# Token-major three-pass retention, and the recurrence one head later, in a two-block layer kernel

## Chip, cores and metric

One core of one Trainium2 chip. The metric is the device time of one execution in microseconds; the kernel before was run three times, 1894.63 to 1899.74 us, median 1894.76.

## What is computed

A batch of one, 512 tokens, width 1024, everything in fp32. Block one: adaptive norm, a projection into seven streams, a causal convolution and gated linear recurrence (RG-LRU), stick-breaking attention in eight heads, a gated mix, `w_out`, then a convolved GELU feed-forward. Block two: a layer with latent attention and multiscale pooling, then a retention layer and a final norm. The two pieces that the change touches:

```python
# block one, per head of 128 channels
log_a = -RG_C * r * softplus(-lam); a = exp(log_a)
u = sqrt(-expm1(2.0 * log_a)) * (i * x)
h = a_t * h + u_t                      # scan over the 512 tokens
y_a = h * gelu(yr)
...
log_beta = log_sigmoid(z)              # z = q k^T / sqrt(d)
suffix = reverse cumsum(log_1mb) - log_1mb
y_b = where(mask, exp(log_beta + suffix), 0) @ v
mix = sigmoid(ga) * y_a + sigmoid(gb) * y_b
# block two, retention, 4 heads with dk = 256, dv = 512, forward and backward decays
scores = (q k^T) * dmat ;  o = scores @ v
y = groupnorm(o) * gn_g * silu(gate) ;  y @ w_out
```

## The kernel before

The engines run hand-written queues tied by semaphores. Activations lie channel-major (channels on partitions, 512 tokens in the free dimension). The weights come as 286 *units* of up to 1024 rows by 128 columns (`UNITS`, made by `ring_plan`). SyncE loads a unit into one of three slots of `raw`, ScalarE copies it to fp32r as the high half (`split_ahead`, L852, at most two units ahead of the one it reads), GpSimd subtracts to get the low half (L478), and TensorE's `unit` (L511 to L513) multiplies in three passes per 128 rows: high by high, high by low, low by high, 24 matmuls of 512 columns for a full unit. Each unit writes a PSUM bank; `bank_plan` deals them in turns from a ring of two banks (`lin`) or, for the kinds in `WIDE`, of five, and a unit first waits until the reader of the bank's previous unit has finished (`BEFORE`, `FREED`).

Block one is a loop of nine steps h. Step h runs the seven units of head h (q, k, v, xr, yr, ga, gb) and the attention of head g = h - 1:

- TensorE: q(h), scores of g into `big` (L602), k(h), v(h), square sum of q in `m_a` (`square`, L532), xr(h), suffix sums of g (L627, L629), square sum of k, yr(h), four transposes of v(h) (L640), ga(h), gb(h), the two gate matmuls of head h (L650, L655), the product attention by v of g into `m_o` (L660). On even steps 16 one-column matmuls of the modulation (L549) stand ahead of the suffixes.
- ScalarE: Abs, Exp, Ln of the scores (L940 to L944), roots of the square sums (L864, L867), Sigmoid of ga, then Sigmoid and Tanh of the recurrence gate (L985, L987), Sigmoid of gb (L992, waits for `mixed`), of the input gate (L995), Sqrt (L999).
- VectorE: shifted logs of g and their split, five lines from L1313 to L1324; one accumulation of the modulation (L1213, weights in `ada_ring`), q norm, convolution of xr(h), L1345, k norm, mask (L1359); then it waits for `av_done` and mixes head g (L1362 to L1368); then decay and recurrence of head h (L1373 to L1394) and the last accumulation.

Step 8 holds only the attention of head 7, with the first seven eighths of the units w_out 0 and 1 laid between its pieces; their last eighth needs `mixed` of head 7.

In a retention head the units are rq, rk (2 each), rv (4), rgate (4). v comes out channel-major, ScalarE copies each unit to SBUF, four fp32 transposes turn it (L797) and ScalarE copies it back as `v_tk`. VectorE rotates q and k. The scores (L809) and the output (L817) are full fp32 matmuls:

```python
for k in range(2):
    last = nc.tensor.matmul(big[:, (4 * h + j) % 3], rk_r[:, k, j * P:(j + 1) * P], rq_r[:, k],
                            start=(k == 0), stop=(k == 1))
...
last = nc.tensor.matmul(ro_bank[b], s_sb[:, j, b * P:(b + 1) * P], v_tk[:, j],
                        start=(j == 0), stop=(j == TB - 1))
```

The scores are multiplied by the decay table on VectorE (L1668). A full fp32 matmul stands in the trace as two records.

## Time and profile before

| | |
|---|---|
| median of three runs | 1894.76 us |
| profiled execution | 1894.31 us |
| its span | 1892.5 us |
| TensorE matmul busy | 1766.3 us, 93% |
| VectorE, ScalarE, GpSimd busy | 944.1, 842.3, 681.6 us |
| mean granted TensorE clock | 0.975 |

The share of busy time is an average over stages, and a matmul's recorded end is modelled: consecutive matmuls overlap in the records, so lengths are best read from starts. Idle time in a row is the time in which the engine stood before that instruction, with what it waited for. Times in a row count from the span's start.

### The profile page before, as it was taken

Reading aid. Unit: us, or ns where it says so; the run is one execution under the profiler, and the core shown is the slowest. Engines: PE = TensorE matmul, PEld = TensorE weight load, DVE = VectorE, ACT = ScalarE, POOL = GpSimd, SP = SyncE. Lnnn points to the kernel's source line nnn. Section 1 sums busy time; section 2 is a strip of 40 time slices with the busy share of each in tenths; the row PEclk is TensorE's granted clock in tenths of the full one; section 3 lists DMA queues with packets and bytes.
Section 4 is the critical chain, followed back from the end, with each engine's and each line's share of the span. In section 5 each row is a group of like instructions: output and inputs, shape, how many; then the busy total and the mean of one; then the engine's idle time right before and its main releaser. Section 6 shows DMA issues by size and latency. Waiting matters only on the chain.

```text
span 1892.5 us, 19419 instructions
## 1 busy us (share of the span) xinstructions
PE 1766.3 (93%) x7336; PEld 1342.9 (71%) x7336; DVE 944.1 (50%) x1137; ACT 842.3 (45%) x1034; POOL 681.6 (36%) x322
## 2 busy tenths in 40 slices
PE   4999999998779999999998989999999999999997
PEld 2777777776557787788786768555578686786765
DVE  6567776666447718525523662344435252233432
ACT  3577666766234424323443321455534343233432
POOL 1333333323244444444452444112244242441424
PEclk7999999999799999999999999999999999999998
DMA  9233332322112232232221222111223121221312
GB/s 364 90 122 101 112 119 83 122 101 74 55 67 90 89 100 90 89 115 98 90 99 50 87 97 67 48 37 37 70 68 100 45 90 56 90 95 39 100 34 78
DMA packets 50350, 168.19 MB, mean 89 GB/s; under 512 B 5585, under 2 KB 10833, under 8 KB 49745
## 3 DMA queue, kind: packets, MB, share of 16 engines
q1 hardware_dynamic: 50256, 166.95, 26.3%
q8 instruction: 59, 0.97, 0.2%
q14 instruction: 35, 0.28, 0.0%
HBM read 164.83 MB, written 2.10 MB: 88 GB/s over the span
## 4 chain that ended last, share of the span: by engine, by line
PE 72%; DVE 22%; ACT 3%; issue 2%; POOL 1%; DMA 1%; SPq 0%; DVEq 0%; ACTq 0%
PE lin L511 18%; PE lin L513 17%; PE lin L512 17%; PE big L817 2%; PE big L754 2%; PE big L753 2%; PE m_o L770 1%; PE big L809 1%; DVE scr L1213 1%; PE big L511 1%; DVE cq_lo L1324 1%; DVE tmp L1375 1%; PE big L512 1%; PE big L513 1%; DVE scr L1320 1%
## 5 line engine op out<-in xcount | busy, mean ns | idle before, releaser
L478 POOL TENSOR_TENSOR w_lo<-raw,w_hi 128x1024 fp32r<-128x1024 f32 (+3 forms) x286 | 640.5, 2243 | 1161.5 <-ACT w_hi L852 1161.4
L511 PE MATMUL lin<-h_hi,w_hi 128*128 128x512 f32 x1328 | 532.7, 401 | 21.6 <-POOL w_lo L478 11.6
L513 PE MATMUL lin<-h_hi,w_lo 128*128 128x512 f32 x1328 | 518.9, 391 | 0.0
L512 PE MATMUL lin<-h_lo,w_hi 128*128 128x512 f32 x1328 | 518.2, 390 | 0.0
L852 ACT ACTIVATE w_hi<-raw 128x1024 fp32r<-128x1024 f32 (+3 forms) x286 | 277.6, 971 | 184.0 <-DVE x L1476 72.0
L511 PEld LDWEIGHTS lin<-h_hi,w_hi 128*128 128x128 f32 x1328 | 250.2, 188 | 89.6 <-POOL w_lo L478 20.5
L512 PEld LDWEIGHTS lin<-h_lo,w_hi 128*128 128x128 f32 x1328 | 250.3, 188 | 54.7 <-issue 5.0
L513 PEld LDWEIGHTS lin<-h_hi,w_lo 128*128 128x128 f32 x1328 | 250.0, 188 | 53.3
L511 PE MATMUL lin<-y_hi,w_hi 128*128 128x512 f32 x484 | 190.9, 394 | 15.3 <-DVE y_lo L1469 4.5
L513 PE MATMUL lin<-y_hi,w_lo 128*128 128x512 f32 x484 | 189.1, 391 | 0.0
L512 PE MATMUL lin<-y_lo,w_hi 128*128 128x512 f32 x484 | 188.9, 390 | 0.0
L511 PEld LDWEIGHTS lin<-y_hi,w_hi 128*128 128x128 f32 x484 | 91.2, 188 | 39.5 <-issue 6.5
L1458 DVE SCALAR_TENSOR_TENSOR scr<-lin,par,scr 128x511 f32<-128x511 f32 x96 | 72.0, 750 | 82.8 <-ACT scr L1018 62.7
L513 PEld LDWEIGHTS lin<-y_hi,w_lo 128*128 128x128 f32 x484 | 91.1, 188 | 19.2
L512 PEld LDWEIGHTS lin<-y_lo,w_hi 128*128 128x128 f32 x484 | 91.3, 189 | 18.7 <-issue 0.2
L1644 DVE TENSOR_TENSOR scr<-lin,rstd 128x512 f32<-128x512 f32 x16 | 11.1, 692 | 132.9 <-PE lin L513 132.9
L1476 DVE SCALAR_TENSOR_TENSOR x<-lin,small,x 128x512 f32<-128x512 f32 x24 | 18.0, 751 | 88.5 <-PE lin L513 88.5
L1018 ACT ACTIVATE scr<-lin,par 128x512 f32<-128x512 f32 x24 | 18.7, 780 | 82.3 <-PE lin L513 82.3
L1014 ACT ACTIVATE scr<-lin,par 128x512 f32<-128x512 f32 x24 | 18.7, 780 | 64.6 <-PE lin L513 62.0
L1702 DVE TENSOR_TENSOR x<-lin,x 128x512 f32<-128x512 f32 x16 | 11.1, 692 | 63.3 <-PE lin L513 63.3
L511 PE MATMUL big<-h_hi,w_hi 128*128 128x512 f32 x96 | 37.7, 393 | 4.7 <-POOL w_lo L478 4.7
L817 PE MATMUL big<-scr 128*128 128x512 f32 x96 | 41.9, 592 | 0.0
(276 smaller groups left out, 2350.4 us busy)
## 6 DMA issues: line engine op xcount, KB each, us to landing
raw<-weights SPq DMA_DIRECT2D x246, 512.0 KB, 3.5
ada_ring<-ada SPq DMA_DIRECT2D x32, 512.0 KB, 4.2
scr<-ada SPq DMA_DIRECT2D x16, 512.0 KB, 6.3
raw<-weights SPq DMA_DIRECT2D x16, 192.0 KB, 2.3
x<-x_t SPq DMA_DIRECT2D x2, 1024.0 KB, 6.0
out_t<-scr SPq DMA_DIRECT2D x8, 256.0 KB, 2.0
rgw<-rg_w SPq DMA_DIRECT2D x1, 1024.0 KB, 6.5
scr<-inv_counts SPq DMA_DIRECT2D x1, 1024.0 KB, 5.8
```

Of the source, the lines that this page charges most:

```text
L478: nc.gpsimd.tensor_tensor(w_lo[:, s, 0:w], raw[:, s, 0:w], w_hi[:, s, 0:w].bitcast(F32), ALU.subtract).then_inc(w_split, 1)
L511: nc.tensor.matmul(psum_of(n), wh, hi(k), start=(k == 0), stop=False)
L512: nc.tensor.matmul(psum_of(n), wh, lo(k), start=False, stop=False)
L513: last = nc.tensor.matmul(psum_of(n), wl, hi(k), start=False, stop=(k == nk - 1))
L753: nc.tensor.matmul(big[:, q % 3], qn_sb[:, cols], kn_sb[:], start=True, stop=False)
L754: nc.tensor.matmul(big[:, q % 3], qrr[rows, h // 2, cols], krr[rows], start=False, stop=True, tile_position=(64 * (h % 2), 0)).then_inc(s_ ...
L770: last = nc.tensor.matmul(m_o[:], vtok[:, g % 2, j], p_t[:, j], start=(j == 0), stop=(j == TB - 1))
L809: last = nc.tensor.matmul(big[:, (4 * h + j) % 3], rk_r[:, k, j * P:(j + 1) * P], rq_r[:, k], start=(k == 0), stop=(k == 1))
L817: last = nc.tensor.matmul(ro_bank[b], s_sb[:, j, b * P:(b + 1) * P], v_tk[:, j], start=(j == 0), stop=(j == TB - 1))
L852: nc.scalar.activation(w_hi[:, s, 0:wd], raw[:, s, 0:wd], ACT.Copy).then_inc(w_high, 1)
L1213: v.scalar_tensor_tensor(out=acc, in0=src, scalar=p_("c", k), in1=acc, op0=M, op1=AD).then_inc(ada_used, 1)
L1458: v.scalar_tensor_tensor(out=o[:, s:T], in0=psum_of(n)[:, 0:T - s], scalar=p_("ffn_conv_w", 48 * (2 - s) + half + c), in1=o[:, s:T], op0=M ...
```

## The change

**Retention.** The rv units become `value_unit`: the activations are the stationary operand and 512 weight columns move, so that v comes out token-major in four banks at once (`rv_bank`), with no transposes. q, k, v and the decayed scores are each split into a high and a low half (ScalarE copies, VectorE subtracts), and scores and output run in three passes of fp32r. The old wait for `yr_ready` is gone; the value units wait for `on_done` and `yrp_done` of the head before.

**Block one.** Head h's xr, yr, ga, gb and its recurrence move from step h to step h + 1, beside the attention of the same head. The wait for `av_done` and the mixing move behind the recurrence. Head 0's second square sum goes to `m_b`. In step 1, k stands ahead of the scores. The last head's tail is written out by itself. `w_out` joins `WIDE`, and rv units take no turn in the bank rings.

The core of the diff (the loading order of `ring_plan` follows the new order of units; the weight array of an rv unit is 256 rows by 512 columns):

```diff
-WIDE = ("kr", "cq", "ckv", "u", "pool", "pgate", "p_out")
+WIDE = ("w_out", "kr", "cq", "ckv", "u", "pool", "pgate", "p_out")
...
+        if kind == "rv":
+            continue
         ring = 5 if kind in WIDE else 2
...
+        rv_bank = [big[:, 2], m_o[:], m_a[:], m_b[:]]
...
+            def value_unit(h, c):
+                n = UNIT[("rv", 4 * h + c)]
+                s = n % NR
+                pe.wait_ge(w_split, n + 1)
+                for k in (2 * c, 2 * c + 1):
+                    at = (k % 2) * T
+                    wh, wl = w_hi[:, s, at:at + T], w_lo[:, s, at:at + T]
+                    for b in range(TB):
+                        hh, hl = h_hi[:, k, b * P:(b + 1) * P], h_lo[:, k, b * P:(b + 1) * P]
+                        nc.tensor.matmul(rv_bank[b], hh, wh, start=(k == 0), stop=False)
+                        nc.tensor.matmul(rv_bank[b], hh, wl, start=False, stop=False)
+                        last = nc.tensor.matmul(rv_bank[b], hl, wh, start=False, stop=(k == DK - 1))
+                last.then_inc(unit_done, 1)
...
+                for c in range(4):
+                    value_unit(h, c)
+                unit("rgate", 4 * h, H, L)
+                pe.wait_ge(rqk_low, 4 * h + 4)
+                pe.wait_ge(rv_low, 4 * h + 1)
...
+                        kh, kl = k_hi[:, k, j * P:(j + 1) * P], k_lo[:, k, j * P:(j + 1) * P]
+                        nc.tensor.matmul(out, kh, q_hi[:, k], start=(k == 0), stop=False)
+                        nc.tensor.matmul(out, kh, q_lo[:, k], start=False, stop=False)
+                        last = nc.tensor.matmul(out, kl, q_hi[:, k], start=False, stop=(k == 1))
                     last.then_inc(rs_scores, 1)
                 unit("rgate", 4 * h + 1, H, L)
-                pe.wait_ge(rs_done, 4 * h + 4)
-                pe.wait_ge(rvt_copied, 4 * h + 4)
+                pe.wait_ge(rs_low, 4 * h + 4)
+                pe.wait_ge(rv_low, 4 * h + 4)
...
+                        nc.tensor.matmul(ro_bank[b], sh, v_hi[:, j], start=(j == 0), stop=False)
+                        nc.tensor.matmul(ro_bank[b], sh, v_lo[:, j], start=False, stop=False)
+                        last = nc.tensor.matmul(ro_bank[b], sl, v_hi[:, j], start=False, stop=(j == TB - 1))
...
+            g = HEADS - 1
+            unit("xr", g, H, L)
+            pe.wait_ge(kq_normed, 2 * HEADS)
+            pe.wait_ge(gates_read, g)
+            scores(g)
+            unit("yr", g, H, L)
+            modulation(5)
+            pe.wait_ge(conv_done, HEADS)
+            nc.tensor.matmul(m_a[:], rgw[:, g], A(S1["xr"], g), start=True, stop=True).then_inc(gate_r_done, 1)
+            unit("ga", g, H, L)
+            pe.wait_ge(lm_done, HEADS)
+            suffixes()
+            unit("gb", g, H, L)
+            pe.wait_ge(att_t, HEADS)
+            nc.tensor.matmul(big[:, 2], rgw[:, 8 + g], A(S1["xr"], g), start=True, stop=True).then_inc(gates_done, 1)
+            for m in range(2):
+                unit("w_out", m, YH, YL, ready=None if m else lambda k: (mixed, k + 1), part=range(7))
+            pe.wait_ge(att_done, HEADS)
+            products(g)
```

VectorE in the loop of block one before, a middle head, from the mask to the next head's logs (`m_o` is the product, `tmp` the recurrence):

```order
L1359 TENSOR_TENSOR scr<-scr,cst 128x128 x4
L1362 TENSOR_TENSOR tmp<-m_o,scr 128x512
L1364 TENSOR_TENSOR tmp<-tmp,scr 128x512
L1366 CAST y_hi<-tmp 128x512
L1368 TENSOR_TENSOR y_lo<-tmp,y_hi 128x512
L1373 TENSOR_SCALAR tmp<-tmp 128x512
```

The same place in the changed kernel (line numbers are its own):

```order
L1453 TENSOR_TENSOR scr<-scr,cst 128x128 x4
L1459 TENSOR_SCALAR tmp<-tmp 128x512
L1461 RECIPROCAL tmp<-tmp 128x512
L1467 TENSOR_TENSOR tmp<-tmp,scr 128x512
L1470 SCALAR_TENSOR_TENSOR tmp<-tmp 128x512
L1473 TENSOR_TENSOR tmp<-tmp 128x512
L1475 TENSOR_SCALAR tmp<-tmp 128x512
L1477 SCALAR_TENSOR_TENSOR tmp<-tmp 128x512
L1480 TENSOR_TENSOR tmp<-tmp,scr 128x512
L1483 TENSOR_TENSOR scr<-tmp,scr 128x512
L1487 TENSOR_TENSOR tmp<-m_o,scr 128x512
L1489 TENSOR_TENSOR tmp<-tmp,scr 128x512
```

The read of `m_o` has moved from the place right behind the mask to the end of the recurrence.

VectorE in a retention head before, from the last rotation to the first statistics (L1644 scales a gate unit, L1668 is the decayed score):

```order
L1493 TENSOR_TENSOR scr<-scr,tmp 128x512
L1644 TENSOR_TENSOR scr<-lin,rstd 128x512
L1668 SCALAR_TENSOR_TENSOR scr<-big,small,tmp 128x512 x4
L1644 TENSOR_TENSOR scr<-lin,rstd 128x512
L1675 BN_STATS small<-m_o 128x6
```

And in the changed kernel (`qk_hl` holds the halves of q and k, `cq_lo` the low half of v):

```order
L1641 TENSOR_TENSOR scr<-scr,tmp 128x512
L1813 TENSOR_TENSOR qk_hl<-scr,qk_hl 128x512 x4
L1817 TENSOR_TENSOR cq_lo<-big,cq_hi 128x512
L1817 TENSOR_TENSOR cq_lo<-m_o,cq_hi 128x512
L1817 TENSOR_TENSOR cq_lo<-m_a,cq_hi 128x512
L1817 TENSOR_TENSOR cq_lo<-m_b,cq_hi 128x512
L1792 TENSOR_TENSOR scr<-lin,rstd 128x512
L1824 SCALAR_TENSOR_TENSOR tmp<-big,small,tmp 128x512 x2
L1830 TENSOR_TENSOR s_lo<-tmp,s_hi 128x512
L1824 SCALAR_TENSOR_TENSOR tmp<-big,small,tmp 128x512
```

Twelve subtractions are new in each head, and the score products alternate with four of them.

## Rows read from the trace of the kernel before

**Rows 1.** The page, busy times and costliest groups: busy, mean ns, idle before.

```profile
PE 1766.3 (93%) x7336; PEld 1342.9 (71%) x7336; DVE 944.1 (50%) x1137; ACT 842.3 (45%) x1034; POOL 681.6 (36%) x322
...
L478 POOL TENSOR_TENSOR w_lo<-raw,w_hi 128x1024 fp32r<-128x1024 f32 (+3 forms) x286 | 640.5, 2243 | 1161.5 <-ACT w_hi L852 1161.4
...
L511 PEld LDWEIGHTS lin<-h_hi,w_hi 128*128 128x128 f32 x1328 | 250.2, 188 | 89.6 <-POOL w_lo L478 20.5
```

**Rows 2.** Waits of TensorE: us in total, times, longest us.

```profile
PE big L627 <- DVE cq_lo L1324: 13.8, 7, 4.8
```

**Rows 3.** Timeline of TensorE, heads in the loop: start, us, instruction, idle before.

```profile
190.77 1.02 PE L650 MATMUL m_a<-scr,rgw 128*128 128x512 f32 x2
...
222.57 0.50 PE L627 MATMUL big<-cq_hi,sel_r 128*128 128x512 f32 x1 [2.35 <-DVE cq_lo L1324]
...
244.71 1.02 PE L650 MATMUL m_a<-scr,rgw 128*128 128x512 f32 x2
```

**Rows 4.** Timeline of VectorE, same heads, and one earlier row.

```profile
113.51 1.49 DVE L1324 TENSOR_TENSOR cq_lo<-scr,cq_hi 128x1280 fp32r<-128x1280 f32 x1
...
194.91 0.69 DVE L1362 TENSOR_TENSOR tmp<-m_o,scr 128x512 f32<-128x512 f32 x1 [9.41 <-PE m_o L660]
...
198.66 0.43 DVE L1373 TENSOR_SCALAR tmp<-tmp 128x512 f32<-128x512 f32 x1
...
211.40 1.49 DVE L1313 SCALAR_TENSOR_TENSOR scr<-big,scr 128x1280 f32<-128x1280 f32 x1
...
218.84 3.68 DVE L1324 TENSOR_TENSOR cq_lo<-scr,cq_hi 128x1280 fp32r<-128x1280 f32 x1
```

**Rows 5.** Timeline of ScalarE, same heads.

```profile
209.57 1.28 ACT L944 ACTIVATE scr<-scr 128x1280 f32<-128x1280 f32 x1
...
246.54 0.72 ACT L987 ACTIVATE tmp<-tmp,small 128x512 f32<-128x512 f32 x1
```

**Rows 6.** Windows: length, busy (x) of PE, PEld, DVE, ACT, POOL, granted clock, DMA.

```profile
125.00:446.00 321.00, 311.39 (x1347) 243.97 (x1347) 221.84 (x215) 214.23 (x229) 106.06 (x43) 0.98 0.32 107
461.00:510.00 49.00, 29.80 (x106) 22.25 (x105) 32.63 (x36) 16.68 (x16) 7.98 (x3) 0.73 0.10 32
1433.00:1870.00 437.00, 431.59 (x1790) 324.52 (x1789) 159.63 (x213) 158.57 (x200) 156.47 (x66) 1.00 0.22 70
```

**Rows 7.** Timeline of TensorE, end of the last head.

```profile
465.67 4.08 PE L602 MATMUL big<-scr 128*128 128x512 f32 x8 [4.29 <-ACT tmp L995]
...
487.90 0.79 PE L627 MATMUL big<-cq_hi,sel_r 128*128 128x512 f32 x1 [4.79 <-DVE cq_lo L1324]
...
498.95 4.64 PE L660 MATMUL m_o<-scr,vtok 128*128 128x512 f32 x8 [5.67 <-DVE scr L1359]
...
506.44 0.47 PE L511 MATMUL lin<-y_hi,w_hi 128*128 128x512 f32 x1 [2.86 <-DVE y_lo L1368]
```

**Rows 8.** Timeline of TensorE, first head, behind the v unit.

```profile
65.74 1.02 PE L532 MATMUL m_a<-sq_act,cst 128*128 128x512 f32 x2
```

**Rows 9.** Timeline of TensorE, third retention head.

```profile
1678.88 0.39 PE L511 MATMUL lin<-h_hi,w_hi 128*128 128x512 f32 x1
...
1684.33 0.60 PE L797 MATMUL m_a<-cst,scr 128*128 128x128 f32 x4
...
1690.26 0.60 PE L797 MATMUL m_b<-cst,scr 128*128 128x128 f32 x4
...
1714.86 3.59 PE L817 MATMUL m_o<-scr 128*128 128x512 f32 x8
...
1718.29 7.03 PE L817 MATMUL big<-scr 128*128 128x512 f32 x16
```

**Rows 10.** Timeline of ScalarE, table load and weight split, first retention head.

```profile
1477.05 1.28 ACT L907 ACT_TABLE_LOAD   x1 [4.39 <-DVE scr L1644]
...
1479.64 1.06 ACT L852 ACTIVATE w_hi<-raw 128x1024 fp32r<-128x1024 f32 x1
```

**Rows 11.** Timeline of VectorE, a score product, first retention head.

```profile
1478.47 0.75 DVE L1668 SCALAR_TENSOR_TENSOR scr<-big,small,tmp 128x512 f32<-128x512 f32 x1 [1.49 <-PE big L809]
```

More of the change, by code:

```diff
@@ L527, in YL, with square @@
                 return y_lo[:, k]
-            def square(count, first, last):
+            def square(count, first, last, out=m_a[:]):
                 pe.wait_ge(squared, count)
-                nc.tensor.matmul(m_a[:], c_("ones"), sq_act[:, count % 2], start=first, stop=last)\
+                nc.tensor.matmul(out, c_("ones"), sq_act[:, count % 2], start=first, stop=last)\
                     .then_inc(square_used, 1)
@@ L597, in _ @@
                     unit("q", h, H, L)
+                if h == 1:
+                    unit("k", h, H, L)
                 if g >= 0:
                     pe.wait_ge(kq_normed, 2 * g + 2)
-                    pe.wait_ge(gates_read, g + 1)
-                    for j in range(TB):
-                        last = nc.tensor.matmul(big_f[:, COL[j]:COL[j] + KW[j]],
-                                                A(S1["k"], g)[:, j * P:(j + 1) * P], A(S1["q"], g)[:, j * P:T],
-                                                start=True, stop=True)
-                    last.then_inc(z_done, 1)
-                if h == HEADS:
-                    unit("w_out", 0, YH, YL, ready=lambda k: (mixed, k + 1), part=range(7))
-                if 0 < h < HEADS:
+                    if g > 0:
+                        pe.wait_ge(gates_read, g)
+                    scores(g)
+                if h > 1:
                     unit("k", h, H, L)
@@ L658, in _ @@
                     pe.wait_ge(att_done, g + 1)
-                    for j in range(TB):
-                        last = nc.tensor.matmul(m_o[:, j * P:T], vtok[:, g % 2, j],
-                                                att_a[:, COL[j]:COL[j] + KW[j]],
-                                                start=(j == 0), stop=(j == TB - 1))
-                    last.then_inc(av_done, 1)
+                    if h < HEADS:
+                        pe.wait_ge(vt_copied, h + 1)
+                    products(g)
+            g = HEADS - 1
+            unit("xr", g, H, L)
+            pe.wait_ge(kq_normed, 2 * HEADS)
+            pe.wait_ge(gates_read, g)
+            scores(g)
+            unit("yr", g, H, L)
+            modulation(5)
+            pe.wait_ge(rgw_loaded, 16)
+            pe.wait_ge(conv_done, HEADS)
+            pe.wait_ge(rooted, 2 * HEADS)
+            nc.tensor.matmul(m_a[:], rgw[:, g], A(S1["xr"], g), start=True, stop=True).then_inc(gate_r_done, 1)
+            unit("ga", g, H, L)
+            pe.wait_ge(lm_done, HEADS)
+            suffixes()
+            unit("gb", g, H, L)
+            pe.wait_ge(att_t, HEADS)
[3 more added lines that the diff above has]
+            pe.wait_ge(att_done, HEADS)
+            products(g)
             pe.wait_ge(gates_read, HEADS)
@@ L928, in _ @@
             highs(0)
-            for h in range(HEADS + 1):
+            for h in range(HEADS):
                 g = h - 1
-                if h == HEADS:
-                    split_ahead(UNIT[("w_out", 0)])
                 if h < HEADS:
@@ L1308, in _ @@
+            for h in range(HEADS):
                 g = h - 1
```

450 lines of the change are left out of this document (274 added, 176 removed).

## Prediction

> **What bounds the kernel now.** I read the page first: TensorE is busy for 93% of the span [rows 1], and nearly all of it is three-pass units, so only two things can move the time: TensorE work that disappears, and TensorE waits (with the slow clock that follows them). Next I read the list of waits for TensorE: one line of the first block stands out, the suffix sums waiting for VectorE's last attention operand, 13.8 us in seven waits [rows 2]. The timelines of the three engines around one head [rows 3 to 5] show why, the windows [rows 6] show the clock, the timeline of the last head's end [rows 7] shows the largest hole, and that of a retention head [rows 9] shows what a matmul costs in each number format.
>
> **The change part by part.**
>
> *Retention, arithmetic.* A unit takes 5.45 us (from its start at 1678.88 to the transposes behind it at 1684.33), that is 24 reduced-precision (fp32r) matmuls of 512 columns at 0.227 us. With the four value transposes it is 5.93 (1684.33 to 1690.26), so a group of transposes costs 0.48; a full fp32 matmul is two records, and eight records take 3.43 us (1714.86 to 1718.29), 0.429 each [rows 9]. Per head the change removes 4 groups of transposes, 4 x 0.48 = 1.92. The scores were 8 fp32 matmuls, 16 x 0.429 = 6.86, and become 24 x 0.227 = 5.45: 1.41 less. The output was 16 matmuls, 32 x 0.429 = 13.72, and becomes 48 x 0.227 = 10.9: 2.82 less. The value units keep 96 matmuls of 512 columns; only which operand is stationary changes. That is 6.15 us per head, **-24.6 us** for four. No TensorE wait stands in this stage that could have swallowed it: TensorE is busy 431.6 of 437 us at full clock [rows 6].
>
> *Retention, new waits.* The scores now wait for the split q and k and for the first value bank, the output for the split scores. Let e be the end of the last value unit. ScalarE has one weight split and four copies to make, VectorE four subtractions; the first value bank is free at about e+2.5, and rgate 0 covers TensorE until e+5.44. q and k are split during the value units. Behind the scores: VectorE scales rgate 0, ScalarE loads a table (1.28) and does the silu and a weight split (1.06) [rows 10], so the first score copy ends near e+10.1. Then VectorE needs four score products (0.75) [rows 11] and four subtractions (about 0.7), ending near e+14.5 undisturbed. rgate 1 covers TensorE until e+16.3. A VectorE operation that meets GpSimd's split can grow: the last attention subtraction took 1.49 undisturbed and 3.68 in another head [rows 4], 2.2 more, which is one GpSimd operation (mean 2.243) [rows 1]. One such hit gives e+16.7. I put **+0.5 us** for the stage; two hits in every head would give 4 x 2.6 = 10, and the bound below is nothing.
>
> Were each of the four score subtractions hit, the path would grow by 4 x 2.2 against a slack of 16.3 - 14.5 = 1.8, and the stage would lose 4 x 7.0 = 28 us, all of its gain. GpSimd has only one split to make in that stretch, so I keep one hit. The Trainium skill, page "SBUF — State Buffer", section "two separate sides", says that VectorE operations with two SBUF inputs and GpSimd operations take a shared port pair as an exclusive lock for the whole instruction, so that all four are exposed; the trace agrees on the size of a hit, 2.2 us.
>
> *Head loop, heads 2 to 7.* Today VectorE sits idle 9.41 us for the products of the head before, mixes (194.91 to 198.66, 3.75 us), and only then runs decay, recurrence and one more accumulation (198.66 to 211.40, 12.7 us), and the shifted logs [rows 4]. Their last subtraction ends at 222.52 and TensorE has stood 2.35 us [rows 3]. After the change decay waits only for the tanh of the gate. It ends 2.55 us after its gate matmul starts (244.71 to 247.26) [rows 3, 5], so at 193.3 in the head shown; 12.7 + 3.75 puts the shifted logs at about 209.8. ScalarE's Ln ended at 210.85 [rows 5], but it also waited for the mixing (its sigmoid of gb) and moves up by about 1.8. So the logs start 1.6 to 2.4 us earlier, and the last subtraction leaves the GpSimd operation that it met (3.68 against 1.49). The wait goes. What these waits cost: 13.8 - 4.79 = 9.0 us in six heads, 1.0 for ends that are modelled 0.16 late, and (1 - 0.98) x 321 = 6.4 us of half clock after them [rows 2, 3, 6, 7]; 16.4 in all. The modulation's one-column matmuls stay beside the suffixes in every second head and may still lower the clock once or twice, so I take **-14.5 us** (ends -6 and -17). VectorE's products are no longer late for anybody: their wait moves behind the recurrence.
>
> *The end of the last head.* Between 461 and 510 us TensorE is idle 49 - 29.8 = 19.2 us; the clock's mean of 0.73 means 26.5 us at half speed, of which the waits of 4.79 and 5.67 hold 10.5, so 16 us of matmuls lose 8 [rows 6, 7]. That is 27.2 us over the work. The new order lays xr, yr, ga, gb (21.8 us of units that were done earlier before) between the pieces. I followed the three engines from the last loop gate matmul (t = 0). VectorE: 2.55 + 12.7 + 3.75 is 19 at the latest, against TensorE's arrival at the modulation at 16.9: 1 to 2 us of wait; the convolution then holds the gate matmul some 0.5. The shifted logs (6.7 undisturbed, 11.1 with the hits of [rows 4]) follow from 20.3: the suffixes wait 0.5 to 4.5. The last mixing must follow products and both w_out parts: about 2.9 us, as now (2.86) [rows 7]. Sum 5 to 10, with half-clock pieces 7 to 13. I take 9: **-18 us** (ends -14 and -22).
>
> *The start.* Head 0's q, k, v stand alone, the v unit ending at 65.74 [rows 8]. Then: two square sums 1.7, q and k of head 1 10.9, scores 2.15, v 5.44: TensorE asks for xr at 87. Its weight split, however, is queued on ScalarE behind Abs, Exp, Ln (three times 1.28 [rows 5] and two table loads of 1.28, from 81 to 87.4), then takes 1.06 there [rows 10] and 2.24 on GpSimd: 90.8. That is 3.8 us of new wait; the suffixes behind it may wait another 0 to 1.7, and the clock may fall: **+6.5 us** (ends +3.5 and +9). The second square sum's own bank saves nothing visible: it lets ScalarE's two roots follow each other, and they are covered by q and k.
>
> *Banks.* w_out joins the five-bank ring, which shifts the later turns: qr 0 now inherits its bank from the last p_out instead of the sixth, and waits for that residual: **+1 us**.
>
> **Sum.** -24.6 + 0.5 - 14.5 - 18 + 6.5 + 1 = -49.1. The profiled execution took 1894.31 us for a span of 1892.5, 0.45 under the median of the runs shown; so 1894.8 - 49.1 = 1845.7, say 1845.
>
> **Rivals.** *Scores split too late* (10 in 100): two GpSimd hits in every retention head, +10: 1855; with all four hit, +28: 1873 (2 in 100). For it: 3.68 against 1.49 [rows 4]. Against: one split in that stretch. *The head loop keeps its waits* (12 in 100): the recurrence, now ahead of the mixing, meets three GpSimd splits (each +2.2) and the logs start no earlier; then the head loop gives nothing and the end of the last head 14: 1845 + 14.5 + 4 = 1863 or so. For it: the same enlarged row; against: the 9.41 us of idle time that VectorE gets back. *Start and end cost less* (7 in 100): +3.5 and -22 in place of +6.5 and -18, 1838. *Weight load exposed, slower than before* (3 in 100): the value units now keep activations stationary, and the scores and outputs issue many more loads. A load takes 0.188 us [rows 1] and is hidden under the matmul today, as 0.227 per matmul shows. There are 4 x (96 + 24 + 48) = 672 such matmuls; if the load stood bare they would cost 126 us: 1971. It decides from 49/672 = 0.07 us per matmul. Against it: units already change their stationary operand with every weight half. *It nets out* (2 in 100).
>
> **How the numbers follow.** The forecast holds 64 in 100 with 1840 to 1851 of its own. To hold eight in ten the range reaches down to 1837 and up to 1860, which takes in the first rival and the middle of the second. Below 0.3% (5.7 us) two runs of this kernel can't be told apart; everything but the last two cases is faster by more: 0.95, 0.02, 0.03.
>
> **What would show it.** Retention: scores begin to rgate 1 in 5.4 us, outputs 10.9, no wait over 0.5 before the outputs. Head loop: no wait of the suffixes in heads 2 to 7, heads without modulation near 49.7 us apart, VectorE's wait for the products under 1 us. Start: one wait near 87 us for GpSimd's split of xr 0. End: four waits of which the last, before w_out's eighth block, is near 3. I would be wrong if the shifted logs are still late, if the outputs wait for split scores, or if a value unit takes more than 5.5 us.

## The result and the profile after

| | before | after |
|---|---|---|
| median | 1896.17 us (4 runs) | 1834.41 us (4 runs, 1830.78 to 1836.63) |
| ratio | | 0.9667, interval 0.965 to 0.9685 |
| profiled execution, span | 1894.31, 1892.5 us | 1834.91, 1833.1 us |
| granted clock, mean | 0.975 | 0.982 |

The change is worth 61.8 us, where 49.8 (1894.8 to 1845) were forecast; 1834.4 lies 2.6 us under the range's lower end. The span shrank by 59.4 us; the rest is scatter between executions.

The page of the changed kernel, TensorE's busy time and GpSimd's weight splits; compare [rows 1]:

```profile
PE 1728.7 (94%) x7368; PEld 1347.4 (74%) x7368; DVE 984.1 (54%) x1185; ACT 852.9 (47%) x1050; POOL 684.9 (37%) x322
L508 POOL TENSOR_TENSOR w_lo<-raw,w_hi 128x1024 fp32r<-128x1024 f32 (+3 forms) x286 | 643.8, 2254 | 1098.1 <-ACT w_hi L924 1097.8
```

The list of TensorE's waits (total us, times, longest). The line of the suffix sums, 13.8 us in [rows 2], has gone from it altogether; those below are the block-one waits that the prediction speaks of, but for the one at the start (its row stands further below), and the one of qr 0 (the third row):

```profile
PE lin L541 <- DVE y_lo L1493: 2.8, 1, 2.8
PE m_b L594 <- DVE small L1330: 1.0, 1, 1.0
PE lin L541 <- DVE x L1734: 0.9, 1, 0.9
PE m_a L734 <- issue: 0.5, 1, 0.5
```

**The six heads of the loop.** The windows of before, then of after, from the second group of value transposes to the eighth (length, busy time of each engine with its instructions, granted clock, DMA):

```profile
125.49:446.01 320.52, 310.91 (x1346) 243.65 (x1345) 221.39 (x214) 213.94 (x228) 105.95 (x43) 0.98 0.32 107
```

```profile
106.65:407.23 300.58, 300.58 (x1345) 238.56 (x1344) 207.80 (x214) 213.93 (x228) 107.99 (x43) 1.00 0.34 114
```

After, TensorE is busy for every one of the 300.58 us, at full clock. VectorE does the same 214 pieces in 13.6 us less, and the groups by line in these windows show where: the last attention subtraction, before and after (busy us, mean ns).

```profile
L1324 DVE TENSOR_TENSOR cq_lo<-scr,cq_hi 128x1280 fp32r<-128x1280 f32 x6 | 22.1, 3683 | 0.2
```

```profile
L1434 DVE TENSOR_TENSOR cq_lo<-scr,cq_hi 128x1280 fp32r<-128x1280 f32 x6 | 9.0, 1492 | 0.2
```

It grew beside GpSimd's split in all six heads and grows in none. The shifted logs of the head that answers to [rows 4], on VectorE, and TensorE's first suffix sum behind them:

```profile
187.32 1.49 DVE L1423 SCALAR_TENSOR_TENSOR scr<-big,scr 128x1280 f32<-128x1280 f32 x1
...
194.84 1.49 DVE L1434 TENSOR_TENSOR cq_lo<-scr,cq_hi 128x1280 fp32r<-128x1280 f32 x1
196.37 3.43 DVE L1326 SCALAR_TENSOR_TENSOR scr<-slab,par,scr 128x1024 f32<-128x1024 f32 x1
```

```profile
197.76 0.39 PE L651 MATMUL big<-cq_hi,sel_r 128*128 128x512 f32 x1
```

The last subtraction takes 1.49 us, as forecast; it ends at 196.33 and TensorE comes at 197.76: 1.4 us of room. In the three heads in which the modulation's matmuls stand ahead of the suffixes it is 3.1 us. GpSimd's weight split beside that subtraction, before and after:

```profile
218.80 2.37 POOL L478 TENSOR_TENSOR w_lo<-raw,w_hi 128x1024 fp32r<-128x1024 f32 x1 [1.99 <-ACT w_hi L852]
```

```profile
196.32 2.39 POOL L508 TENSOR_TENSOR w_lo<-raw,w_hi 128x1024 fp32r<-128x1024 f32 x1 [3.18 <-ACT w_hi L924]
```

Before, the split began 0.04 us ahead of the subtraction (218.84 in [rows 4]). Now it begins 0.02 us before the subtraction ends, in all six heads. In three of them the accumulation behind the subtraction grows in its place (3.43 against 1.28); in the other three VectorE has nothing to do there. The shifted logs start 4.1 us ahead of the square sum that stands before xr (187.32 and 191.41) where they started 1.95 us ahead of it (211.40 and 213.35), while ScalarE makes its half of this split behind the root of that same square sum. The mask additions met GpSimd's split before (3.50 us for four) and meet it still (3.58).

**The start and the last head**, TensorE's rows that waited (compare [rows 7]):

```profile
90.40 0.76 PE L541 MATMUL lin<-h_hi,w_hi 128*128 128x512 f32 x1 [2.49 <-POOL w_lo L508]
...
436.68 1.95 PE L594 MATMUL m_b<-cst,scr 128*128 128x1 f32 x16 [0.95 <-DVE small L1330]
439.08 2.04 PE L734 MATMUL m_a<-scr,rgw 128*128 128x512 f32 x2 [0.45 <-issue]
...
470.75 0.47 PE L541 MATMUL lin<-y_hi,w_hi 128*128 128x512 f32 x1 [2.85 <-DVE y_lo L1493]
```

The clock was 0.50 for 3.4 us behind the first and behind the third of them:

```profile
90.50:93.90 3.40, 3.40 (x8) 2.68 (x9) 3.27 (x4) 3.31 (x5) 2.23 (x1) 0.50 0.45 153
438.60:442.00 3.40, 2.95 (x6) 1.72 (x6) 3.33 (x3) 1.93 (x3) 1.69 (x1) 0.50 0.18 27
```

**Retention**, VectorE's score splits in one head, and TensorE's first output:

```profile
1658.36 2.26 DVE L1830 TENSOR_TENSOR s_lo<-tmp,s_hi 128x512 fp32r<-128x512 f32 x1 [1.09 <-ACT s_hi L1270]
...
1661.44 0.69 DVE L1830 TENSOR_TENSOR s_lo<-tmp,s_hi 128x512 fp32r<-128x512 f32 x1
...
1662.95 1.49 DVE L1830 TENSOR_TENSOR s_lo<-tmp,s_hi 128x512 fp32r<-128x512 f32 x2
```

```profile
1664.49 0.50 PE L888 MATMUL m_o<-cq_hi,s_hi 128*128 128x512 f32 x1
```

Of the four subtractions one was hit (2.26 against 0.69) in each of the four heads, as the forecast's sum has it, with 1.6 us and not 2.2. The last ends at 1664.44, and TensorE starts 0.05 us later. No idle time is listed, but the output starts 0.31 us after the matmul ahead of it (1664.18) where matmuls of one unit follow each other in 0.23: it waited for the split, by 0.08 us, in each head.

Where the 59.4 us of span are, by landmarks of both traces:

| stretch | before | after | measured | forecast |
|---|---|---|---|---|
| start (from the end of head 0's v unit to the second group of value transposes) | 36.2 | 40.4 | +4.2 | +6.5 |
| six heads of the loop | 320.5 | 300.6 | -19.9 | -14.5 |
| end of the last head (from the eighth group to the next norm's sum) | 119.7 | 97.6 | -22.1 | -18 |
| qr 0 | | | +1.1 | +1 |
| retention, from the third norm's sum to the last norm's | 448.8 | 424.6 | -24.2 | -24.1 |
| rest of the kernel | | | +1.6 | 0 |

Four units and two gate matmuls (4 x 5.45 + 2 x 0.86 = 23.5 us) have moved from the first stretch to the third. To compare the same work, they are taken off the start before (59.75 as it stands in the trace) and added to the end before (96.2).

### The profile page after: what moved, and what is told of

The parts are those of the page before. It is cut to its first block, busy times and chain, and to the rows that moved or that the text cites. A ratio compares the mean times of both kernels' runs of the same rounds, so it can differ in the third digit from the quotient of the medians.

```text
span 1833.1 us, 19563 instructions
## 1 busy us (share of the span) xinstructions
PE 1728.7 (94%) x7368; PEld 1347.4 (74%) x7368; DVE 984.1 (54%) x1185; ACT 852.9 (47%) x1050; POOL 684.9 (37%) x322
## 4 chain that ended last, share of the span: by engine, by line
PE 80%; DVE 13%; ACT 3%; issue 2%; POOL 1%; DMA 1%; SPq 0%; DVEq 0%; ACTq 0%
PE lin L541 19%; PE lin L543 18%; PE lin L542 18%; PE big L835 2%; PE big L541 2%; PE big L542 2%; PE big L543 2%; PE big L834 2%; PE m_o L851 2%; DVE tmp L1350 1%; POOL w_lo L508 1%; DVE scr L1606 1%; DVE scr L1326 1%; DVE scr L1702 1%; PE m_o L660 1%
## 5 line engine op out<-in xcount | busy, mean ns | idle before, releaser
L541 PE MATMUL lin<-h_hi,w_hi 128*128 128x512 f32 x1192 | 477.5, 401 | 22.7 <-POOL w_lo L508 13.3
L542 PE MATMUL lin<-h_lo,w_hi 128*128 128x512 f32 x1192 | 466.5, 391 | 0.0
L543 PE MATMUL lin<-h_hi,w_lo 128*128 128x512 f32 x1192 | 466.5, 391 | 0.0
L541 PEld LDWEIGHTS lin<-h_hi,w_hi 128*128 128x128 f32 x1192 | 225.2, 189 | 80.6 <-issue 18.4
L542 PEld LDWEIGHTS lin<-h_lo,w_hi 128*128 128x128 f32 x1192 | 225.4, 189 | 48.8 <-issue 3.9
L543 PEld LDWEIGHTS lin<-h_hi,w_lo 128*128 128x128 f32 x1192 | 225.1, 189 | 47.7
L542 PE MATMUL lin<-y_lo,w_hi 128*128 128x512 f32 x446 | 174.3, 391 | 0.0
L543 PE MATMUL lin<-y_hi,w_lo 128*128 128x512 f32 x446 | 174.3, 391 | 0.0
L1326 DVE SCALAR_TENSOR_TENSOR scr<-slab,par,scr 128x1024 f32<-128x1024 f32 x28 | 46.4, 1658 | 1.0
L1749 DVE TENSOR_REDUCE small<-big 128x1 f32<-128x512 f32 x32 | 22.1, 692 | 39.5 <-PE big L835 39.5
```

What stands on the lines that cost most here:

```text
L541: nc.tensor.matmul(psum_of(n), wh, hi(k), start=(k == 0), stop=False)
L542: nc.tensor.matmul(psum_of(n), wh, lo(k), start=False, stop=False)
L543: last = nc.tensor.matmul(psum_of(n), wl, hi(k), start=False, stop=(k == nk - 1))
L1326: v.scalar_tensor_tensor(out=acc, in0=src, scalar=p_("c", k), in1=acc, op0=M, op1=AD).then_inc(ada_used, 1)
L1749: v.reduce_max(sm(STAT + 8), big[:, q % 3], AX_X).then_inc(dve_order, 1)
```

## The experiments

All ratios are to the kernel before, from runs on the same chip. After stands for the changed kernel, 0.9667.

**1. Retention alone (ret_only).** Block one and the banks as before, the retention part of the change kept:

```diff
+        if kind == "rv":
+            continue
...
+                for c in range(4):
+                    value_unit(h, c)
+                unit("rgate", 4 * h, H, L)
+                pe.wait_ge(rqk_low, 4 * h + 4)
+                pe.wait_ge(rv_low, 4 * h + 1)
...
```

> The kernel before with the retention part of the change alone: block one is in the old order, w_out in the two-bank ring; value units token by token and scores and outputs in three passes are kept. Theory A (the retention terms stand by themselves, as rows 9 price them): 24.1 us less than the kernel before (-23 to -26), the last root-mean-square sum to the end of the kernel as in the changed kernel, block one as before. Theory B (the gain of the whole change beyond my sum came from retention, or retention and block one help each other through the clock): more than 30 us less, or less than 20. Every time in block one should be within 0.5 us of the kernel before.

1873.35 us, 0.9868 (0.9851 to 0.9886): 24.4 less than before's 1897.77 on that chip. The window from the third norm to the fourth, in this kernel and in the changed one, is the same to 0.02 us:

```profile
1434.77:1859.32 424.55, 419.46 (x1870) 344.67 (x1869) 213.91 (x262) 173.35 (x220) 160.42 (x68) 1.00 0.23 74
```

```profile
1394.14:1818.71 424.57, 419.57 (x1869) 344.75 (x1868) 213.88 (x262) 173.11 (x220) 160.27 (x68) 1.00 0.24 74
```

The retention term stands by itself. The excess is in block one. That block one would repeat to 0.5 us was wrong: the six heads took 322.3 us against 320.5, with a fifth half-clock stretch, and the feed-forward 432.5 against 429.1, both with the instructions of before. That the medians give just the 24 us is therefore in part luck; the window is the evidence.

**2. VectorE's order alone (order_only).** The kernel before, with the mixing of head g behind the recurrence of head h, and sigmoid of gb in two buffers in turns:

```diff
-                    dve.wait_ge(av_done, g + 1)
-                    v.tensor_tensor(tmp[:, 3], m_o[:], SGB, M).then_inc(dve_order, 1)
...
+                if g >= 0:
+                    dve.wait_ge(av_done, g + 1)
+                    v.tensor_tensor(tmp[:, 3], m_o[:], GB(g), M).then_inc(dve_order, 1)
...
-                    if h > 0:
-                        act.wait_ge(mixed, h)
-                    nc.scalar.activation(SGB, i, ACT.Sigmoid).then_inc(gb_done, 1)
+                    if h > 1:
+                        act.wait_ge(mixed, h - 1)
+                    nc.scalar.activation(GB(h), i, ACT.Sigmoid).then_inc(gb_done, 1)
```

> The kernel before with one thing changed in block one: VectorE runs decay and recurrence of head h ahead of the mixing of head h-1, which needs a second buffer for the sigmoid of gb. No shift by one head, no own order at the end, the start and retention are those of before. Theory A (VectorE's order is what removed the suffix waits; the shift by a head is only how it was arranged): the six suffix waits vanish, head loop -20 us (-15 to -20), the end of the last head -5, no loss at the start: -22 to -25 in all. Theory B (the shift is needed, because ScalarE or the gates hold VectorE up elsewhere): waits stay or move to another place, and the gain is under 10 us.

1874.13 us, 0.9875 (0.986 to 0.989), 23.6 less. The six heads take exactly what they take after the whole change:

```profile
125.42:426.00 300.58, 300.58 (x1345) 238.44 (x1344) 207.97 (x214) 214.08 (x228) 108.62 (x43) 1.00 0.34 114
```

So the loop's gain is VectorE's order, with the second buffer that it needs, and nothing else; the shift by one head costs the start and serves the end. Here the end of the last head gains only 4.5 us, and waits of 5.2, 3.0, 5.7 and 2.9 us are left in it.

**3. The last head in the loop's order (loop_tail).** The changed kernel, with its last head issued as a step of the loop would be (TensorE's part; the queues of ScalarE and VectorE follow it):

```diff
-            unit("xr", g, H, L)
             pe.wait_ge(kq_normed, 2 * HEADS)
             pe.wait_ge(gates_read, g)
             scores(g)
+            unit("xr", g, H, L)
+            modulation(5)
+            pe.wait_ge(lm_done, HEADS)
+            suffixes()
             unit("yr", g, H, L)
-            modulation(5)
+            unit("ga", g, H, L)
+            unit("gb", g, H, L)
...
```

> The changed kernel with the last head's tail in the loop's plain order (scores, xr, modulation, suffixes, yr, ga, gb, both gate matmuls, w_out in two parts, products). Theory A (the pieces laid between cover VectorE's chain): the suffixes wait 13 us or more for the shifted logs and w_out's last block waits 5 to 9 us for the last mixing, so 15 to 25 us slower than the changed kernel, with two or three half-clock stretches. Theory B (the end got shorter only because the recurrence no longer stands ahead of the logs, and its own order adds little): under 5 us slower than the changed kernel.

1844.86 us, 0.9723 (0.9707 to 0.974), 10.5 us slower than after. TensorE's waits in the stretch:

```profile
PE big L651 <- DVE cq_lo L1434: 5.1, 1, 5.1
PE lin L541 <- DVE y_lo L1493: 3.1, 1, 3.1
PE m_b L594 <- DVE small L1330: 3.0, 1, 3.0
PE big L640 <- ACT tmp L1066: 1.1, 1, 1.1
```

Between the two theories: 12.3 us of waits in place of 4.3, the rest clock. Theory A's 13 us for the suffixes were too much: waits of 9.2 us stand in three places (scores 1.1, modulation 3.0, suffixes 5.1), and the last mixing costs 3.1 and not 5 to 9. The last head's own order is worth 10 of the 22 us.

**4. The first head's second square sum (sq_shared).**

```diff
-                    square(8 + 2, True, True, m_b[:])
+                    pe.wait_ge(rooted, 1)
+                    square(8 + 2, True, True)
...
-                    root(P, rooted, of=m_a[:] if h else m_b[:])
+                    root(P, rooted, of=m_a[:])
```

> The changed kernel with the first head's second square sum back in the shared bank m_a, so that TensorE has to wait for ScalarE's first root before it starts the second. Theory A (what my prediction says, that the own bank saves nothing visible): within 1 us of the changed kernel. Theory B (TensorE stands still there, since nothing is laid between the two sums any more): the first sum ends near 67, ScalarE's Ln and Exp need about 2.9 us with a table load, so TensorE waits 3 to 4.5 us at 67 and perhaps loses 1.7 at half clock: 3 to 6 us slower than the changed kernel.

1840.66 us, 0.97 (0.9685 to 0.9714), some 6 us slower than after. TensorE, and below it ScalarE's root:

```profile
65.81 1.02 PE L577 MATMUL m_a<-sq_act,cst 128*128 128x512 f32 x2
70.88 2.08 PE L577 MATMUL m_a<-sq_act,cst 128*128 128x512 f32 x2 [4.06 <-ACT rstd L940]
```

```profile
66.91 1.28 ACT L937 ACT_TABLE_LOAD   x1 [0.24 <-PE m_a L577]
68.20 0.69 ACT L937 ACTIVATE rstd<-m_a,eps 128x512 f32<-128x512 f32 x1
68.91 1.28 ACT L940 ACT_TABLE_LOAD   x1
70.20 0.63 ACT L940 ACTIVATE rstd<-rstd 128x512 f32<-128x512 f32 x1
```

Theory B: 4.1 us of wait, then a slow clock. "Saves nothing visible" was wrong. It did not enter the sum, because the changed kernel has the bank of its own.

**5 and 6. The start: k's copy, or only the weight split, ahead of Abs (fix_start, start_split).** First the edit of fix_start, then that of start_split:

```diff
+                    if h == 1:
+                        i = at("k", h)
+                        nc.scalar.activation(A(S1["k"], h), i, ACT.Copy).then_inc(k_copied, 1)
+                        act.wait_ge(k_copied, counted(k_copied))
+                        square(10 + 2 * h, A(S1["k"], h))
...
```

```diff
+                if h == 1:
+                    split_ahead(UNIT[("k", 1)])
                 if g >= 0:
                     act.wait_ge(z_done, g + 1)
                     nc.scalar.activation(att_a, big_f[:, 0:1280], ACT.Abs).then_inc(act_order, 1)
```

> The changed kernel with the copy and the square of head 1's k ahead of Abs, Exp, Ln on ScalarE, so that the weight split of xr 0 is issued before them too. Theory A (the start's loss is the one wait of 2.5 us for GpSimd's w_lo near 88-90 us and the half clock behind it): that wait goes, the second value transposes start 4.2 us earlier (102.5 in place of 106.65), and block one is 4.3 us shorter. Theory B (the loss is in the longer chain at the start itself; the wait moves to the suffix sums, whose logs are now later): under 1 us.

> The changed kernel with one ScalarE operation moved: the weight split of xr 0 is issued ahead of Abs, Exp, Ln of head 0, in ScalarE's idle time of 2.5 us before Abs (the copy of k stays behind them). Theory A (the start has two equal chains, split and logs, and k's bank is a third): GpSimd's low part is ready near 84, xr 0 then waits only for the copy of k near 88.5 in place of 90.4, and VectorE's mask additions, which met GpSimd there, are 2.2 us shorter, so the shifted logs end near 94 and are no wait; the second value transposes start 1.5 to 2 us earlier. Theory B (as in the run that moved the copy too: the logs get later): 2 to 3 us slower at that place.

1839.76 (0.9709, 0.9693 to 0.9725) and 1839.84 us (0.9707, 0.9689 to 0.9724): both 5 to 8 us slower than after. The wait for the split is gone and a longer one for the logs is there, in fix_start and in start_split:

```profile
97.35 0.79 PE L651 MATMUL big<-cq_hi,sel_r 128*128 128x512 f32 x1 [4.39 <-DVE cq_lo L1440]
```

```profile
97.56 0.80 PE L651 MATMUL big<-cq_hi,sel_r 128*128 128x512 f32 x1 [4.12 <-DVE cq_lo L1436]
```

```profile
93.85 3.65 DVE L1436 TENSOR_TENSOR cq_lo<-scr,cq_hi 128x1280 fp32r<-128x1280 f32 x1
```

The last row is start_split's VectorE. Split and logs are two chains of one length: in fix_tail below, whose start is that of the changed kernel and whose clock stays up there, the logs end at 95.80 and the suffixes begin at 95.85. In the changed kernel the logs end at 95.92, and xr 0, at half clock, lasts until 97.57. Moving the split delays the start of the logs by 0.2 us (1.2 with the copy) and moves GpSimd's next operation onto their last subtraction (3.65 against 1.49). By the second group of value transposes, fix_start is 2.6 us behind the changed kernel and start_split 1.6, so theory B was right in kind both times (the logs get later), and in neither in size. Neither of these two orders of ScalarE wins anything at the start.

The rest of the 5 us lies in stages whose instructions are the same: in both kernels the feed-forward takes 3.2 us more and the latent attention 2.6 less, with other half-clock stretches. In start_split the last head takes 2.5 more. GpSimd and VectorE there:

```profile
445.83 2.37 POOL L508 TENSOR_TENSOR w_lo<-raw,w_hi 128x1024 fp32r<-128x1024 f32 x1 [3.91 <-ACT w_hi L924]
```

```profile
445.86 3.68 DVE L1436 TENSOR_TENSOR cq_lo<-scr,cq_hi 128x1280 fp32r<-128x1280 f32 x1
```

The split begins 0.03 us ahead of the last subtraction, and the suffixes wait 2.33 us. In the changed kernel the same split begins 0.9 us after the subtraction has started, which takes 1.49. What differs is the clock: there the gate matmul at 439.08, whose result ScalarE's chain ahead of this split reads, ran at half clock and took 2.04 us, here 1.10.

**7 and 8. The end: products earlier; x gate earlier too (fix_tail, early_gate).** fix_tail moves the products between w_out 0 and 1, and ScalarE's sigmoid of the x gate ahead of that of gb:

```diff
-            for m in range(2):
-                unit("w_out", m, YH, YL, ready=None if m else lambda k: (mixed, k + 1), part=range(7))
+            unit("w_out", 0, YH, YL, ready=lambda k: (mixed, k + 1), part=range(7))
             pe.wait_ge(att_done, HEADS)
             products(g)
+            unit("w_out", 1, YH, YL, part=range(7))
...
```

early_gate also multiplies the x gate behind the r gate and runs the recurrence ahead of the mask:

```diff
+            pe.wait_ge(mixed, g)
+            nc.tensor.matmul(m_o[:], rgw[:, 8 + g], A(S1["xr"], g), start=True, stop=True).then_inc(gates_done, 1)
             unit("ga", g, H, L)
...
-            mask_products()
-            recur(g)
+            recur(g, mask_products)
```

> The changed kernel with the last attention product between w_out 0 and w_out 1, and ScalarE's sigmoid of the x gate ahead of that of gb. Theory A (w_out's last block waits 2.85 us for the last mixing only because the products stand behind both w_out parts): the mixing can start 4.1 us earlier, the wait goes, block one 2.5 to 3 us shorter, or 4 with the half clock. Theory B (the mixing waits for the recurrence of the last head, not for the products): under 0.5 us, or a wait for the masked products in the new place of 1 to 3 us.

> The changed kernel with another last-head tail: the x gate is multiplied right behind the r gate, into m_o, its sigmoid follows at once, VectorE runs the recurrence while ScalarE does the last Exp and masks the attention products behind it, and the products stand between w_out 0 and 1. Theory A (the wait of 2.8 us before w_out's eighth block is VectorE's recurrence, which waits for the x gate; the run that only moved the products left it at 2.6): recurrence starts near 453 in place of 459.6, the last mixing follows the products at once and ends before TensorE asks for it; that wait goes, block one 2.5 to 3 us shorter, with half-clock time up to 4.5. Theory B (GpSimd's splits of the w_out weights stretch VectorE whatever the order): 1 us or less.

1834.01 (0.9673, 0.9658 to 0.9687) and 1837.11 us (0.9686, 0.9665 to 0.9706). fix_tail is not told apart from after; it leaves the last wait at 2.64, since VectorE is in the recurrence until 466.4, two of its operations having met GpSimd's splits (2.75 and 2.50 us); that was theory B. In early_gate that wait has gone and another stands in front of the products (first row), with GpSimd on the mask multiplications (second row, 3.32 against 1.27). Its last head takes 100.2 us against 97.6, with half clock for 10.2 us in place of 3.4:

```profile
463.14 1.24 PE L660 MATMUL m_o<-scr,slab 128*128 128x512 f32 x2 [2.28 <-DVE scr L1454]
```

```profile
459.67 3.32 DVE L1454 TENSOR_TENSOR scr<-scr,cst 128x128 f32<-128x128 f32 x4
```

**9. Both (both).** start_split and early_gate in one kernel, meant to be faster than the changed one.

> Both edits together (xr 0's split ahead of Abs; the early x gate of the last head). Theory A: block one 4 to 5 us shorter than in the changed kernel, 6 with half-clock time: about 1829 to 1831 where the changed kernel has 1834.4. Theory B (what is gained is given back in the next block, as clock or as wait): within 2 us of the changed kernel.

1839.29 us, 0.9698 (0.9681 to 0.9716): 5 us slower than after, with the 4.1 and the 2.3 us waits of its two parts, outside both theories. No version was faster than the changed kernel.

**10. w_out in the two-bank ring (no_wide).**

```diff
-WIDE = ("w_out", "kr", "cq", "ckv", "u", "pool", "pgate", "p_out")
+WIDE = ("kr", "cq", "ckv", "u", "pool", "pgate", "p_out")
```

> The changed kernel with w_out back in the two-bank ring. Theory A (as predicted: the ring's shift gives the first qr unit the bank of the last p_out, 1.07 us of wait there, and w_out itself needs no more than two banks): about 1 us faster, all of it at qr 0. Theory B (w_out needs the banks): waits for VectorE's residual within the eight w_out units, 1 to 4 us slower.

1836.17 us, 0.9691 (0.9675 to 0.9708): not told apart from after. The wait of 0.9 at qr 0 is gone, and no wait stands in w_out that was not there, so both parts of theory A hold in the trace, though its 1 us is not seen in the total; the feed-forward, whose instructions are untouched, took 3.2 us longer at a lower clock. In the changed kernel and in this one:

```profile
504.84:933.94 429.10, 405.64 (x1758) 330.64 (x1756) 237.08 (x259) 164.79 (x188) 194.76 (x84) 0.99 0.29 92
```

```profile
504.07:936.41 432.34, 408.86 (x1757) 332.87 (x1756) 237.05 (x259) 164.81 (x188) 194.89 (x84) 0.98 0.29 92
```

**11. Late logs (late_logs).** The low part of the logs subtracted four times, 4.5 us more per head:

```diff
-                v.tensor_tensor(lm_lo, att_b, lm_hi.bitcast(F32), SU).then_inc(lm_done, 1)
+                for _ in range(3):
+                    v.tensor_tensor(lm_lo, att_b, lm_hi.bitcast(F32), SU).then_inc(dve_order, 1)
+                    dve.wait_ge(dve_order, counted(dve_order))
+                v.tensor_tensor(lm_lo, att_b, lm_hi.bitcast(F32), SU).then_inc(lm_done, 1)
```

> The changed kernel with the subtraction of the shifted logs' low part done four times in place of once, some 4.5 us more on VectorE in each of the eight heads, nothing else. It shows what a wait of the suffix sums costs with all that follows it. Slack today is about 1.4 us, so 2 to 4 us of wait for each of heads 1 to 7, 13 to 20 in all. Theory A (my reading of before: each such wait also brings a half-clock stretch of 3.4 us, 1.7 lost, in the heads without modulation and in those with it): 25 to 33 us slower than the changed kernel. Theory B (the waits cost themselves alone): 13 to 20 us.

1893.84 us (10 runs), 0.9988 (0.9979 to 0.9997): 59 us more than after, so nearly all of the change is given back. TensorE's waits, and the window of the six heads:

```profile
PE big L651 <- DVE cq_lo L1437: 36.5, 8, 5.2
```

```profile
114.28:455.58 341.30, 314.91 (x1345) 250.42 (x1344) 241.43 (x232) 213.99 (x228) 108.00 (x43) 0.95 0.30 101
```

Both theories were too low, as the waits came to 4.6 us each. In every head one of the added subtractions met GpSimd's next split (3.55 to 3.67 us in place of 1.49). So VectorE is 4.5 + 2.2 = 6.7 us later; less the room of 1.4 that is 5.3, where 5.24 was measured, and less the 3.1 of the heads with modulation 3.6, where it was 3.55. In the six heads 26.4 us of wait cost 40.7 us (341.3 against 300.6), as half-clock stretches of 3.4 or 6.8 us come with each wait: a microsecond of wait costs about 1.5. That is theory A's mechanism, with more lost per wait than its 1.7 us (2.4).

**12. The room in the retention (slack).** Each score split's subtraction done twice:

```diff
                         v.tensor_tensor(s_lo[:, j - 1], s_raw[:, (j - 1) % 2], s_hi[:, j - 1].bitcast(F32), SU)\
-                            .then_inc(rs_low, 1)
+                            .then_inc(dve_order, 1)
+                        dve.wait_ge(dve_order, counted(dve_order))
+                        v.tensor_tensor(s_lo[:, j - 1], s_raw[:, (j - 1) % 2], s_hi[:, j - 1].bitcast(F32), SU)\
+                            .then_inc(rs_low, 1)
```

> The changed kernel with each score split's subtraction in the retention done twice, so 4 x 0.7 = 2.9 us more on VectorE in each of the four heads, nothing else. It shows how much room the split scores have. In the changed kernel the last split ends at 1664.4 and the outputs start at 1664.5. Theory A (the score splits are at the limit, one GpSimd hit already has used the room that I counted): 2.9 to 5 us of wait in each head, and half-clock stretches of 3.4 us behind them: 15 to 27 us slower than the changed kernel. Theory B (there is room, rgate 1 covers more than the trace seems to show): under 6 us slower.

1850.14 us, 0.9765 (0.9739 to 0.9791), 16 us more than after by the medians; in the trace 14.4 of it in the retention:

```profile
PE m_o L888 <- DVE s_lo L1833: 11.0, 4, 2.8
```

Theory A, at its lower end, since only two of the four waits brought a half-clock stretch: there is no room at all. The retention's gain is whole because the splits end just in time. Of 2.9 us more on VectorE 2.84 come out in every head (8.36 us from the start of rgate 1 to the outputs, 5.52 after), of which the list shows 2.76 as a wait.

## Why the prediction was right and wrong

**Right.** The sign, and each mechanism at its place: the retention term (-24.1 forecast, -24.2 measured in its window, with the rest of the change and without), with one GpSimd hit and not four; the suffix waits gone in all six heads, with logs 2.1 us earlier against TensorE where 1.6 to 2.4 were forecast; the bank of qr 0; one wait at the start for GpSimd's split of xr 0, due "near 87", there at 87.9 to 90.4; the last wait before w_out's eighth block near 3 (2.85). That retention agrees to 0.1 us is in part chance. TensorE's busy time in the window fell by 23.8 us (443.4 to 419.6). In it are the 0.3 us of new waits (0.08 in each head) where +0.5 was forecast, so the matmuls gave 24.1 and not 24.6; the other 0.4 are listed waits that got shorter. The rivals fell: the outputs waited under 0.1 us a head, the head loop did not keep its waits, and no weight load showed, since the value units kept 5.44 us. VectorE operations on SBUF beside a GpSimd split were up to 2.2 us longer (1.49 to 3.65 or 3.68, 0.69 to 2.26), and one operation paid for one split; the second of the shifted logs, which reads a PSUM bank, kept its 1.49 us at 188.84 with a split from 188.35 to 190.76 beside it. The Trainium skill, page "SBUF — State Buffer", section "two separate sides", says that a VectorE operation with two SBUF inputs and a GpSimd operation that reads SBUF lock the shared ports against each other, and that the one that starts first holds them for its whole instruction. The trace agrees: with the split 0.04 us ahead, the subtraction took 2.2 us more, for a split of mean 2.25; with the split 0.02 us before the subtraction's end, nothing.

**Wrong: the sizes of three terms, all to the same side.**

*Head loop, "I take -14.5 us"; measured -19.9.* Three things were off. First, the reserve of 1.9 for "the modulation's one-column matmuls ... may still lower the clock once or twice": they did not once, the window's clock is 1.00, and the full 16.4 of the forecast's own sum was to be had. Second, that sum lacked a wait which the list of waits does not show. xr's weight split stood behind Ln on ScalarE and then on GpSimd, so that xr began late in every head. GpSimd's two splits in the head of [rows 3] (the first ends at 214.42, 0.06 us before xr's first matmul, and so in all six heads), and TensorE there, before:

```profile
212.02 4.79 POOL L478 TENSOR_TENSOR w_lo<-raw,w_hi 128x1024 fp32r<-128x1024 f32 x2 [6.43 <-ACT w_hi L852]
```

```profile
213.35 1.02 PE L532 MATMUL m_a<-sq_act,cst 128*128 128x512 f32 x2
214.48 0.50 PE L511 MATMUL lin<-h_hi,w_hi 128*128 128x512 f32 x1
214.81 0.39 PE L512 MATMUL lin<-h_lo,w_hi 128*128 128x512 f32 x1
```

and after:

```profile
191.41 1.02 PE L577 MATMUL m_a<-sq_act,cst 128*128 128x512 f32 x2
191.87 0.79 PE L541 MATMUL lin<-h_hi,w_hi 128*128 128x512 f32 x1
192.50 0.39 PE L542 MATMUL lin<-h_lo,w_hi 128*128 128x512 f32 x1
```

From the square sum to xr's second matmul it was 1.46 us and is 1.09: 0.37 in each of six heads, 2.2 us, with no idle time listed, since the modelled end of the square sum covers all but 0.1 of the gap. The forecast had even noted that ScalarE "moves up by about 1.8", and used it only for the logs. Third, the half clock of [rows 6] is four stretches of 3.4 us (from 169.1, 223.7, 329.5 and 384.1), 6.8 lost and not 6.4. 16.4 + 2.2 + 0.4 = 19.0; 0.9 us is left unassigned.

*The end of the last head, -18; measured -22.1.* The forecast's new waits were 1 to 2 at the modulation (0.95), some 0.5 at the gate (0.45), 0.5 to 4.5 at the suffixes (none, so three waits where it said four) and 2.9 at the last mixing (2.85). The suffix term is the one that failed: the logs took the 6.7 us of the undisturbed case and ended at 445.7, 1.2 us ahead of TensorE, since no operation of theirs grew beside GpSimd. That was luck. In start_split, with the same instructions there, the split came 0.03 us ahead of the last subtraction, the suffixes waited 2.33 us, inside the 0.5 to 4.5 of the forecast, and the end took 2.5 us more. Half-clock pieces cost 1.7 and not 2 to 3. So 6.0 are left of the 27.2 where I took 9; a last 0.9 was not assigned.

*The start, +6.5; measured +4.2.* The wait was 2.49 and not 3.8, and the suffixes did not wait. ScalarE's chain had been given two table loads; the trace has one between Abs and the weight split, so the split was ready 24.2 us after the end of the v unit and not 25.1:

```profile
84.25 1.28 ACT L1014 ACT_TABLE_LOAD   x1
```

TensorE asked 21.7 us after it and not 21.3. (The pieces listed in the forecast add up to 85.9; it says 87.) With the half clock (1.7) it is 4.2; in four other kernels (fix_tail, no_wide, early_gate, slack) the same instructions take 1.4 us less, since the clock stays up there.

5.4 + 4.1 + 2.3 is 11.8 us; the rest of the kernel takes 1.6 back, of which 1.2 lie in the latent attention, whose code the change leaves alone and where a half-clock stretch is 6.8 us after and 3.4 before. That gives the 10.3 by which the span falls below the sum of -49.1. For each term I had taken a value inside its bounds, away from the good end, against mishaps that were different ones; three such reserves add up to a forecast that is off by 10 us, and the range had only 8 us below the forecast, since of the rivals one alone, with 7 in 100, was faster.

## What to carry to other kernels

The list of waits shows only idle time in front of a row, and a matmul's modelled end can cover a wait. So compare the distance between the starts of the same two instructions with their undisturbed distance. When one engine's order is changed, follow every queue that moves up with it, not only the one that was the bound. Before a reserve is taken off a term, ask whether the range already holds it; and where two chains have one length, as in the start here, shortening one of them buys nothing. Where a GpSimd split and a VectorE operation start within hundredths of a microsecond of each other, count both outcomes.

## What the runs showed of the hardware

The granted clock is a part of each number that the code does not decide. The feed-forward stage ran the same instructions in all 14 traces, in 428.9 to 429.2 us in eight and 432.3 to 432.5 in six; the difference is two half-clock stretches of 3.4 us. At the start the wait of 2.5 us was followed by one in some kernels and by none in others. Differences under 3 us between these kernels are not readable from the total, only from waits and windows.

Moving an operation on ScalarE moves the GpSimd operation that depends on it, and so which VectorE operation is 2.2 us longer: in fix_start, start_split and early_gate that is where the removed wait came back. The clock does the same: in start_split a gate matmul that kept full clock brought a split forward onto the last subtraction of the last head.
